# First feed-forward block's input product in output halves, with high weights over high and low tokens in one matmul of 512 columns

## The reference, cut to what matters

```
def swiglu(h, w_in, w_out):
    g, u = jnp.split(h @ w_in, 2, axis=-1)        # w_in: 1024 x 5632
    return (jax.nn.silu(g) * u) @ w_out           # w_out: 2816 x 1024
```

## Time and profile before

| | before |
|---|---|
| median of three runs | 1123.02 us |
| the profiled execution's own time | 1122.82 us |
| its span in the trace | 1121.1 us |
| granted TensorE clock, mean | 0.999 |
| PE busy | 1109.9 us, 99% |
| DVE busy | 784.6 us, 70% |
| ACT busy | 584.5 us, 52% |
| bytes read | 234.72 MB, 210 GB/s over the span |
| c = 2 of `in0` begins / `out0` begins | 242.35 / 353.28 us |

### The profile page before, as it was taken

The page is one execution under the profiler, slowest core; times in us unless marked ns, Lnnn a source line. Parts: engine busy times, 40 slices in busy tenths (PEclk is TensorE's granted clock), DMA queues, the critical chain, the costliest instruction groups (busy, mean ns, idle before and its releaser), DMA issues.

```text
span 1121.1 us, 14577 instructions
## 1 busy us (share of the span) xinstructions
PE 1109.9 (99%) x5882; PEld 920.9 (82%) x5882; DVE 784.6 (70%) x928; ACT 584.5 (52%) x825; POOL 62.7 (6%) x121
## 2 busy tenths in 40 slices
PE   8999999999999999999999999999999999999998
PEld 4688767889998887888888878887888888888886
DVE  2497588889799797887654866455657667784454
ACT  3542367554444436655543667455765366654342
POOL 0011130001111101000000000000000000000000
PEclk9999999999999999999999999999999999999999
DMA  9986760769998966795454797786634446555541
GB/s 329 379 294 228 255 172 6 263 220 330 342 351 314 329 203 201 227 301 185 168 207 143 167 236 179 155 171 142 172 113 151 151 150 225 199 193 201 196 160 38
DMA packets 120565, 236.73 MB, mean 211 GB/s; under 512 B 5665, under 2 KB 61282, under 8 KB 120370
## 3 DMA queue, kind: packets, MB, share of 16 engines
q1 hardware_dynamic: 105984, 184.89, 52.9%
q0 software_dynamic: 14224, 50.64, 13.3%
q10 hardware_dynamic: 290, 0.26, 0.1%
HBM read 234.72 MB, written 1.05 MB: 210 GB/s over the span
## 4 chain that ended last, share of the span: by engine, by line
PE 91%; DVE 1%; ACT 1%; issue 0%; ACTq 0%
PE ps L2082 19%; PE ps L2084 19%; PE ps L2083 18%; PE ps L2144 10%; PE ps L2146 5%; PE ps L2124 3%; PE ps L2125 3%; PE ps L2123 3%; PE ps L2261 2%; PE ps L2438 1%; PE ps L2400 1%; PE ps L2311 1%; PE ps L2307 1%; PE ps L2696 0%; PE ps L2675 0%; PE ps L2653 0%
## 5 line engine op out<-in xcount | busy, mean ns | idle before, releaser
L1205 DVE TENSOR_TENSOR wL<-raw,wH 128x1024 fp32r<-128x1024 f32 x326 | 393.8, 1221 | 209.3 <-ACT wH L654 207.4
L654 ACT ACTIVATE wH<-raw 128x1024 fp32r<-128x1024 f32 x326 | 339.1, 1057 | 298.3 <-PE ps L2084 209.1
L2082 PE MATMUL ps<-wH,aHL 128*128 128x512 f32 x576 | 229.0, 398 | 1.0 <-DVE aHL L1639 0.4
L2083 PE MATMUL ps<-wL,aHL 128*128 128x512 f32 (+1 forms) x592 | 228.9, 387 | 0.0
L2084 PE MATMUL ps<-wH,aHL 128*128 128x512 f32 x576 | 224.7, 390 | 0.0
L2144 PE MATMUL ps<-aHL,wH 128*128 128x512 f32 x480 | 169.3, 398 | 0.0
L2082 PEld LDWEIGHTS ps<-wH,aHL 128*128 128x128 f32 x576 | 108.1, 188 | 32.0 <-issue 5.0
L2146 PE MATMUL ps<-aHL,wL 128*128 128x256 f32 x480 | 134.2, 280 | 0.0
L2083 PEld LDWEIGHTS ps<-wL,aHL 128*128 128x128 f32 x592 | 111.3, 188 | 21.1
L2084 PEld LDWEIGHTS ps<-wH,aHL 128*128 128x128 f32 x576 | 108.1, 188 | 23.2
L2144 PEld LDWEIGHTS ps<-aHL,wH 128*128 128x128 f32 x480 | 90.1, 188 | 21.8 <-issue 0.2
(11 more groups left out here) (358 smaller groups left out, 1523.6 us busy)
## 6 DMA issues: line engine op xcount, KB each, us to landing
raw<-in_ffn_w_in SPq DMA_DIRECT2D x88, 512.0 KB
modraw<-in_w_mod POOLq DMA_DIRECT2D x80, 512.0 KB, 6.4
raw<-in_w_in SPq DMA_DIRECT2D x32, 1024.0 KB
raw<-in_ffn_w_out SPq DMA_DIRECT2D x22, 1024.0 KB
raw<-in_w_up SPq DMA_DIRECT2D x16, 1024.0 KB
raw<-in_w_down SPq DMA_DIRECT2D x16, 1024.0 KB
mod<-in_w_mod SPq DMA_DIRECT2D x8, 1024.0 KB, 11.8
raw<-in_attn_w_qkv SPq DMA_DIRECT2D x8, 1024.0 KB
```

The lines of the kernel that those rows point to most:

```text
L654: nc.scalar.activation(wHigh(n), raw[:, (n // 2) % RAW, (n % 2) * 1024:(n % 2) * 1024 + 1024], ACT.Copy).then_inc(w_hi, 1)
L1205: V.tensor_tensor(wL[:, n % WL, :], raw[:, (n // 2) % RAW, (n % 2) * 1024:(n % 2) * 1024 + 1024], wHigh(n).bitcast(fp32), ALU.subtract).th ...
L2082: T.matmul(outp, xh, h, start=first, stop=False, skip_group_check=part_of)
L2083: T.matmul(outp, xh, l, start=False, stop=False, skip_group_check=part_of)
```

## The change

Layer 0 takes the form of layer 1 for c = 2 to 10; `chunk_mm_T` is gone. `in0` has 20 units in place of 11. The modulation steps stay in the same chunks, at their new place behind the gate. The places of `vec_total` in PE's order do not change. `out0` begins with the first token tile of subs 0 and 1, and takes the second tile of both then (`lead=2`). The total of vector 8, behind `out0`, goes to another bank.

```diff
-                      ("in0", 11)
+                      ("in0", 20)
-TOTAL_BANK = {1: 6, 2: 2, 8: 0}
+TOTAL_BANK = {1: 6, 2: 2, 8: 2}
...
 (ACT)           def one(c):
-                    if layer == 1 and c >= 2:
-                        low_half("in1", c, 0, sh[:, :, c % 2, 0, :])
+                    if c >= 2:
+                        low_half(f"in{layer}", c, 0, sh[:, :, c % 2, 0, :])
                     for j in range(3):
                         adv(n + 4 * c + WS + j)
-                    if layer == 1 and c >= 2:
-                        low_half("in1", c, 1, sh[:, :, c % 2, 1, :])
-                        act.wait_ge(acc_out, half_unit_of("in1", c, 1) + 1)
+                    if c >= 2:
+                        low_half(f"in{layer}", c, 1, sh[:, :, c % 2, 1, :])
+                        act.wait_ge(acc_out, half_unit_of(f"in{layer}", c, 1) + 1)
                         src = sil[:, c % 2, :, :]
                     else:
...
                 def high(c):
-                    if layer == 1:
-                        act.wait_ge(gated_done, c - 1)
-                    else:
-                        act.wait_ge(acc_out, un + c + 1)
+                    act.wait_ge(gated_done, HIDDEN[f"in{layer}"] + c - 1)
...
 (DVE)           def one_by_halves(c):
                     sums(c, 0)
...
-                    dve.wait_ge(silu_done, 11 + c + 1)
-                    dve.wait_ge(acc_out, half_unit_of("in1", c, 1) + 1)
+                    dve.wait_ge(silu_done, 11 * layer + c + 1)
+                    dve.wait_ge(acc_out, half_unit_of(f"in{layer}", c, 1) + 1)
                     V.tensor_tensor(hid[:, c % 2, :, :], sil[:, c % 2, :, :], hid[:, c % 2, :, :], ALU.mult).then_inc(gated_done, 1)
                     for j in range(3):
                         beside(c, j)
                 def one(c):
-                    if layer == 1 and c >= 2:
+                    if c >= 2:
                         one_by_halves(c)
                         return
...
 (PE)            for c in range(2, 11):
-                    if layer == 0:
-                        chunk_mm_T(n + 4 * c, un + c, aH, aL)
-                    else:
-                        chunk_mm_halves(n + 4 * c, "in1", c)
+                    chunk_mm_halves(n + 4 * c, f"in{layer}", c)
                     if c == 2:
                         hid_group(1)
                     if layer == 0 and c in FF0_SELECT:
                         vec_total(FF0_SELECT[c])
...
-                        ..., halves=(0, 1) if layer == 0 else (), lead=0 if layer == 0 else 2)
+                        ..., halves=(0, 1) if layer == 0 else (), lead=2)
```

More of the change, by code:

```diff
@@ L73 @@
 _n = 0
-for _name, _count in (("q", 2), ("k", 4), ("v", 4), ("wo", 2), ("in0", 11), ("out0", 2), ("pool", 2),
+for _name, _count in (("q", 2), ("k", 4), ("v", 4), ("wo", 2), ("in0", 20), ("out0", 2), ("pool", 2),
                       ("in1", 20), ("out1", 2), ("win", 16),
@@ L190, in halves_before @@
 def halves_before(stage, c):
-    return (0 if stage == "in1" else 9) + c - 2
+    return HIDDEN[stage] + c - 2
 def slot(n):
@@ L924, in one @@
                         act.wait_ge(w_used, summed(f"in{layer}", c))
-                        if c < 2:
-                            src = pair(un + c)[:, :, 0:256]
-                        else:
-                            src = pair(un + c)[:, 0, :].rearrange("p (t c) -> p t c", t=2)
+                        src = pair(un + c)[:, :, 0:256]
                     nc.scalar.activation(sil[:, c % 2, :, :], src, ACT.Silu).then_inc(silu_done, 1)
@@ L1729, in sums @@
                 def sums(c, half):
-                    dve.wait_ge(low_part, 2 * halves_before("in1", c) + half + 1)
+                    dve.wait_ge(low_part, 2 * halves_before(f"in{layer}", c) + half + 1)
                     part_ = sh[:, :, c % 2, half, :]
-                    V.tensor_tensor(part_, pair(half_unit_of("in1", c, half))[:, :, 0:S], part_, ALU.add).then_inc(acc_out, 1)
+                    V.tensor_tensor(part_, pair(half_unit_of(f"in{layer}", c, half))[:, :, 0:S], part_, ALU.add).then_inc(acc_out, 1)
                 def one_by_halves(c):
@@ L1754, in one @@
                     dve.wait_ge(silu_done, 11 * layer + c + 1)
[L1755 to L1761, removed]
+                    V.tensor_tensor(hid[:, c % 2, :, :], sil[:, c % 2, :, :], pair(un + c)[:, :, 256:512], ALU.mult).then_inc(acc_out, 1)
                     adv(n + 4 * c + WS + 3)
@@ L2108, in chunk_mm @@
                         after_sub(s)
[L2110 to L2126, removed]
             def chunk_mm_halves(n, stage, c):
@@ L2140, in chunk_mm_halves @@
                             for i in range(2):
-                                b = half + 2 * i if stage == "in1" else 2 * half + i
+                                b = 2 * half + i if stage == "up" else half + 2 * i
                                 dst = pair(un)[:, i, :]
@@ L2502, in swiglu @@
                 rows_mm(SUBS[f"out{layer}"], UNITS[f"out{layer}"], hH, hL, F1 // P, None, beside,
-                        hidden=f"in{layer}", hooks=hooks, window=6 if layer == 0 else WS, halves=(0, 1) if layer == 0 else (), lead=0 if layer == 0 else 2)
+                        hidden=f"in{layer}", hooks=hooks, window=6 if layer == 0 else WS, halves=(0, 1) if layer == 0 else (), lead=2)
             swiglu(0, "x1")
```

## The result

The changed kernel takes **1156.69 us** (median of 4 runs, 1156.09 to 1158.97) against 1123.01 for the kernel before: ratio 1.0305, 95% interval 1.0293 to 1.0317. It is slower, and the time lies in the range 1145 to 1158, 4.4 us above the forecast of 1152.3.

The account below looks back on a forecast made before the run. PE, busy 99% of the span, was taken as the bound, so its waits count in full: 30.4 us of waits less 1.9 saved is +28.5 on 1122.8, 1151.3, plus 1.0 for the clock: 1152.3 us, range 1145 to 1158.

Parts of the forecast that it names:

- The bound and the direction: Whole kernel: PE, busy 99%, is the bound; DVE has about 1 us slack per `in0` chunk; slower, chance 0.96.
- DVE's cycle: `in0`: DVE needs 15.0 us for a chunk with three steps and a put, 15.2 with four (14.7 with a first step).
- PE's saving: `in0`, nine chunks: 11.30 instead of 11.51 us each on PE, 0.21 us saved per chunk, -1.9 us in all.
- The waits one by one: `in0` and `out0`: PE waits for DVE's sums and steps at ten places, 30.4 us in all, 12.7 at total 5.
- The clock: Behind PE's waits of 12.7 and 5.2 us: granted clock falls, at most 5.65 us each, 1.0 us taken in all.
- DMA 0: `in0`: late weights cost between 0 and +8.6 us; 0 taken, since DVE then lags more than ACT's weights do.
- Order alone: Rival, `in0` and `out0`: steps fill DVE's idle times, its lag does not build up, 1131 us; chance 0.09.
- Weights late in addition: Rival, `in0`: late weights, or the clock at its upper end, add 8 to 11 us: 1159 to 1162; chance 0.09.
- Faster: Rival, `in0`: all steps' results come in time, step 47 before total 5, PE gains 1.9 us: 1120.9; chance 0.02.

Follow-up runs that it names:

- e5: Changed kernel with layer 0's DVE and ACT work reordered from chunk 2, steps between `adv` and sums, second `finish` tile behind chunk 2: 1132.39 us.
- e12: e11 with the second sum ahead of the chunk's first step and the pool scale's load behind all but the last modulation load: 1122.93 us, ratio 0.9994.
- e4: Changed kernel with unused matmuls of 512 columns on PE, 45 ahead of total 5 and 18 ahead of total 7: 1153.68 us.
- e2: Changed kernel with the modulation steps of chunks 2 to 10 only 8 columns wide, except each vector's first and last: 1140.67 us.
- e1: Changed kernel with layer 0's modulation steps again beside the first three `adv`, ahead of second sum and gate; halves kept: 1145.07 us.
- e6: e5 with the totals of vectors 4, 5 and 6 one chunk later, behind chunks 6, 8 and 10: 1128.05 us.
- e9: Kernel before, its 256-column matmuls and whole chunks kept, with only the modulation steps moved behind the gate and fourth `adv` from chunk 2: 1131.14 us.
- e10: e6 with total 7 two subs of `out0` later: 1126.82 us.
- e11: e10 with e5's order in layer 1 too and the product of sc1b and lnp moved from DVE's first to tenth place in `out0`: 1125.83 us.

## Why the prediction was right, point by point

**The bound and the direction: right.** A form of matmul that PE alone would like was put into a stage where DVE has 1 us of slack per chunk, and in an order that makes DVE wait three times a cycle. Shown by e5: the same instructions in another order take back 24 us.

**DVE's cycle: right.** Forecast 14.7 to 15.2 us; measured, start to start of the first sums from chunk 3 to 7: 14.85, 14.94, 14.67, 14.95.

**PE's saving: right in size, and never seen as a gain.** In e12 chunks 7 and 8 take 330.00 - 305.68 - 1.72 = 22.60 us, 11.30 each as forecast, against 11.51. That is 0.21 us a chunk. The Trainium skill's fixed cost of a matmul ("TensorE: Matmul & The Clock Gate", section "Back-to-back issue gap"), 2.5 ns, which the page gives for an isolated matmul, would make it 0.08; the trace of this stream shows more. The 0.353 us for a pair were seen, and 0.347 too: chunks 3 and 8 to 10 of the changed kernel ran at that distance, 0.2 us a chunk shorter still.

**The waits one by one** (measured as the excess of one start over the normal distance):

| place | forecast us | measured us |
|---|---|---|
| chunk 2's second half | 0 | 0.3 |
| chunk 3 | 1.0 | 1.1 |
| chunk 5 | 2.1 | 2.8 |
| total 4 | 1.7 | 1.45 |
| chunk 6 | 0.3 | 0.1 |
| chunk 7 | 3.4 | 3.3 |
| total 5 | 12.7 | 10.96 |
| chunk 10 | 0.9 | 1.44 |
| `out0` | 1.5 | 1.7 |
| second tile | 1.65 | 1.42 |
| total 7 | 5.2 | 5.2 |
| sum | 30.4 | 29.8 |

Total 5 waited less only since chunk 7 ended 1.6 us later, at half clock; without that the two lists are 30.4 and 31.4.

**The clock: the term that was mis-sized.** "so I take 1.0 in all" should have been 5.65: total 5 took 1.1 us longer and the first matmuls behind it 0.75 (1.85 together), total 7's sixteen matmuls 3.58 - 1.68 = 1.9, and the nine behind them 9 x 0.2 = 1.9. Another 1.6 in chunk 7 were hidden in total 5's wait. The forecast priced only the waits of 12.7 and 5.2 us, left out its own wait of 3.4 us before chunk 7, and took 1.0 for both places together, though its upper end was 5.65 at each. The sum at the pool stage's start: 29.8 + 1.6 + 5.65 - 1.9 = 35.2; it moved from 415.04 to 450.26, 35.2. That the two agree to the tenth is luck: by the trace chunk 2's stretch began 0.3 us later (its transposes at 242.06 instead of 241.75), the four chunks at 347 ns saved 0.8 more, and the missing half us is spread. The span moved by 33.4: 1.8 us come back in the stages behind, 0.85 of them between `in1`'s total and the end of `out1` (513.42 to 617.54 before, 548.52 to 651.79 after), which is the 347 ns again; what gives back the rest, most of it between 879 and 890 us of the kernel before, is open. Without these 1.8 us, which the forecast did not have, the profiled execution would have taken 1158.0 us, the upper end of the range: that the time lies clear of it is luck too. e4 shows the clock's share by itself: 5.16 us at the pool stage, for matmuls without use. The Trainium skill ("TensorE: Matmul & The Clock Gate", section "HAM oscillation — how this bites in real kernels") says that idle gaps cost a second time in the work behind them; the trace agrees, with 5.65 us behind gaps of 11 and 5 us and 1.6 behind one of 3.3.

**What is hidden, DMA 0: right for this kernel, and for a reason that was half seen.** ACT's wait for weights fell from 25.3 to 1.0 us, and the likely reason is that the stage was 23 us longer for the same bytes. In e2 and e12, where DVE keeps up, the weights are 5 us late in chunk 5 (in e5 at most 1.9), and in the new form that reaches PE by way of `adv` and `sums`.

**The rivals.** *Order alone* (1131) wanted the steps to fill DVE's idle times; the order as written forbids it, and e5, which writes it so, took 1132.4. *Weights late in addition* did not come. *Faster* needed a step ahead of chunk 7's gate; it is what e1, with its step 47 beside the `adv`, did at total 5 (0.78 us), and there the loop paid elsewhere.

**Later expectations that missed.** e2 (9 us too low) for the weights; e5 and e6 (9 and 5 us too low at least) since totals 5 and 7 still waited, with the clock on top; e9 (at least 1 us too low) for the clock again: a wait costs its length and something on top. e4 was 2.7 us too low for what `in1` gave back, e10 and e11 3.8 and 3.3 for the modulation row, e12 1.9 for the weights. In e9, 4.1 + 1.1 at total 5, 0.5 behind it, then 0.4 + 1.9 at total 7 make its 8 us.

## What to carry to other kernels

A new form of the bound engine's work moves more than its own cost: here each chunk now asked two sums of DVE before PE could go on, and a loop over three engines ran at 15 us with 12.3 us of DVE's work in it. Write down the closed loop of the new form, with its idle times, and put other work of the same engine in these idle times rather than behind the loop; then look at what was late without harm before (weights here), for in a tighter loop it is late with harm. A wait of the matrix engine is priced with the clock behind it, and a load that must wait for one result should not stand in a queue ahead of loads that another engine needs.

## What was not expected of the hardware

- The granted clock fell after quite short stops. In the changed kernel a wait of 3.3 us before 312.29 was followed by 0.60 and 0.55 until 316; in e9 a wait of 0.26 us with 16 matmuls of two columns behind it by 0.68 and 0.50 from 380 to 384. The kernel before runs the same 16 matmuls without a wait, and its clock reads 1.00 there.
- While it was down, matmuls of 512 columns lay 0.43 us apart instead of 0.23, and total 7's two-column ones took 3.58 us together instead of 1.68. The clock was still at 0.50 behind them; it returned after nine matmuls of 512 columns, in 411 to 413 us.
- The chunk of the new form has two lengths at full clock: in e12 chunks 9 and 10 took 353.91 - 330.00 - 1.72 = 22.19 us together, chunks 7 and 8 22.60. A matmul of 512 columns and its partner of 256 take 353 ns in one and 347 in the other, and half a chunk, 16 pairs, 5.65 or 5.55 us. First and last pair of such a half in `in1`, first in the kernel before, then in the changed one, with the granted clock at 1.00 in both:

```profile
461.95 0.40 PE L2144 MATMUL ps<-aHL,wH 128*128 128x512 f32 x1
467.25 0.40 PE L2144 MATMUL ps<-aHL,wH 128*128 128x512 f32 x1
```

```profile
566.72 0.39 PE L2114 MATMUL ps<-aHL,wH 128*128 128x512 f32 x1
571.92 0.39 PE L2114 MATMUL ps<-aHL,wH 128*128 128x512 f32 x1
```

  In the changed kernel's `in0` the distance changed only where PE had stopped or run something else: 353 ns in chunk 2, 347 in chunk 3, 353 in chunks 4 to 7, 347 from total 5 on. All nine chunks of `in1` in the kernel before ran at 353. What sets it is open, and it is worth up to 1.7 us between two traces of `in1`.
